# A weight stream in loads of two chunks with rows of 8 kB, in a two-block transformer kernel

## The reference

```python
sh1, sc1, gt1, sh2, sc2, gt2 = split(silu(c) @ w_mod + b_mod, 6)
h = rmsnorm(x, g_attn) * (1 + sc1) + sh1          # and the same for ctx
cq, ckv, kr, qn, kn, vn, f = split_columns(h @ w_in)
x = x + gt1 * (concat(o_mla, o_na, o_fn) @ w_out)
x = x + gt2 * conv_ffn(rmsnorm(x, g_ffn) * (1 + sc2) + sh2, w_up, w_down)
x = rmsnorm(x, g_final)
# second block
qa, ka, va, qb, kb, vb, ga, gb = split(rmsnorm(x) @ w_in_2)
x = x + (sigmoid(ga) * (ya @ w_branch_a_2) + sigmoid(gb) * (yb @ w_branch_b_2)) @ w_out_2
x = rmsnorm(x + swiglu(rmsnorm(x), w_ffn_in_2, w_ffn_down_2))
```

## Time and profile before

| | us |
|---|---|
| median of 3 runs | 2613.85 (2613.49 to 2614.14) |
| the profiled execution | 2613.18 |
| its span | 2611.3 |
| PE busy | 2589.2 (99%) |
| DVE busy | 1780.8 (68%) |
| ACT busy | 1219.5 (47%) |
| stream loads | 1016, 540.35 MB on their queue |
| read over the span | 209 GB/s |

### The profile page before, as it was taken

How to read it: one execution, slowest core, us unless ns; L and a number is a source line. 1 busy time by engine, 2 the same in 40 slices (tenths; PEclk the granted TensorE clock), 3 DMA queues, 4 the chain that set the end, 5 groups by cost and what they waited for, 6 DMA issues and landing times.

```text
span 2611.3 us, 37160 instructions
## 1 busy us (share of the span) xinstructions
PE 2589.2 (99%) x15234; PEld 2234.2 (86%) x15234; DVE 1780.8 (68%) x2469; ACT 1219.5 (47%) x1604; POOL 33.4 (1%) x30
## 2 busy tenths in 40 slices
PE   8999999999999999999999999999999999999999
PEld 5788778888888888888888888899888888888888
DVE  3377977888888877555656677676766666665555
ACT  4442445455555555444433555544444444444443
POOL 2100000000000000000000000000000000000000
PEclk9999999999999999999999999999999999999999
DMA  9887975667777655555555544465555555555553
GB/s 391 350 310 270 332 242 179 229 223 237 237 239 235 208 190 185 196 188 193 184 190 187 168 139 143 147 194 194 190 189 191 188 192 188 192 186 194 188 192 122
DMA packets 151561, 547.73 MB, mean 210 GB/s; under 512 B 16992, under 2 KB 18912, under 8 KB 150624
## 3 DMA queue, kind: packets, MB, share of 16 engines
q1 hardware_dynamic: 148752, 540.35, 61.2%
q10 hardware_dynamic: 2640, 5.01, 0.7%
HBM read 542.68 MB, written 2.10 MB: 209 GB/s over the span
## 4 chain that ended last, share of the span: by engine, by line
PE 92%; DVE 5%; DMA 2%; ACT 1%; issue 0%; SPq 0%; ACTq 0%; DVEq 0%
PE ps L481 47%; PE ps L480 24%; PE ps L478 3%; PE ps L485 3%; PE ps L486 3%; PE ps L487 3%; DVE lo L433 1%; DVE raw L444 1%; PE ps L479 1%; PE ps L493 1%; PE ps L492 1%; PE ps L491 1%; PE ps L1708 1%; DMA raw<-in_stream 1%; PE ps L1930 1%; DMA raw_deep<-in_stream 0%
## 5 line engine op out<-in xcount | busy, mean ns | idle before, releaser
L433 DVE TENSOR_TENSOR lo<-raw,hi 128x1024 fp32r<-128x1024 f32 x815 | 992.9, 1224 | 704.4 <-ACT hi L420 702.4
L481 PE MATMUL ps<-pair,hi 128*128 128x512 f32 x3994 | 1390.7, 392 | 0.0
L420 ACT ACTIVATE hi<-raw 128x1024 fp32r<-128x1024 f32 x815 | 860.4, 1059 | 1054.5 <-PE ps L481 894.1
L480 PE MATMUL ps<-pair,lo 128*128 128x256 f32 x3994 | 1119.4, 280 | 0.1
L481 PEld LDWEIGHTS ps<-pair,hi 128*128 128x128 f32 x3994 | 749.9, 188 | 161.2
L480 PEld LDWEIGHTS ps<-pair,lo 128*128 128x128 f32 x3994 | 749.9, 188 | 6.4 <-issue 2.8
L481 PE MATMUL ps<-hid,hi 128*128 128x512 f32 x1376 | 477.4, 392 | 0.0
L480 PE MATMUL ps<-hid,lo 128*128 128x256 f32 x1376 | 384.6, 280 | 0.0
L481 PEld LDWEIGHTS ps<-hid,hi 128*128 128x128 f32 x1376 | 258.3, 188 | 56.7
L480 PEld LDWEIGHTS ps<-hid,lo 128*128 128x128 f32 x1376 | 258.3, 188 | 0.3
L1298 DVE TENSOR_REDUCE tmp<-ps 128x256 f32<-128x512 f32 x260 | 176.6, 684 | 5.0 <-PE ps L481 4.6
(11 more groups left out here) (347 smaller groups left out, 2314.3 us busy)
## 6 DMA issues: line engine op xcount, KB each, us to landing
raw<-in_stream SPq DMA_DIRECT2D x983, 512.0 KB, 4.2
raw_deep<-in_stream SPq DMA_DIRECT2D x31, 512.0 KB, 10.7
xc<-in_xc SPq DMA_DIRECT2D x4, 1024.0 KB, 8.6
x<-in_x ACTq DMA_DIRECT2D x1, 2048.0 KB, 9.3
out<-out_sb SPq DMA_DIRECT2D x8, 256.0 KB, 2.9
c_bc<-in_c_bc SPq DMA_DIRECT2D x1, 1024.0 KB, 10.2
bias<-in_rpb ACTq DMA_DIRECT2D x4, 256.0 KB, 4.7
dft<-in_dft_tab ACTq DMA_DIRECT2D x1, 512.0 KB, 8.0
```

Of the source, the lines that this page charges most:

```text
L420: e.activation(hi[:, c % R, :], raw_of(p), ACT.Copy).then_inc(hi_ready, 1)
L433: e.tensor_tensor(lo[:, c % R, :], raw_of(p), hi[:, c % R, :].bitcast(F32), ALU.subtract)\
L480: e.matmul(out[:, T:2 * T], wlo, act[:, 0, :], start=False, stop=False)
L481: return e.matmul(out, whi, both_, start=False, stop=last)
```

## The change

The stream is laid out in pairs: rows 2t and 2t+1 of the list become one block of [128, 2048], so that each partition's row is 8 kB of contiguous memory. SP issues one DMA for two chunks (`load(t)`), into two neighbouring places, after waiting for both places to be free (`place_free`, twice). The places have one semaphore for two, and the users of both chunks wait for it. The order of chunks, the splits, the dots and the products stay. `N_DEEP` becomes 82, an even number, so that the second kr chunk also gets a place in the ring of 10. The kr chunks are now loaded whole. `vecs` is issued between chunks 3 and 4 and `c_bc` between 47 and 48, as before.

```diff
-N_DEEP = POS[("weights", AT[("a", KT - 1)])] + 1
+N_DEEP = (POS[("weights", AT[("a", KT - 1)])] + 2) // 2 * 2
...
-        landed = [sem(f"landed{i}") for i in range(RR + DEEP)]
+        landed = [sem(f"landed{i}") for i in range((RR + DEEP) // 2)]
...
-                e.wait_ge(landed[PLACE[p]], 16 * NTH[p])
+                e.wait_ge(landed[PLACE[p] // 2], 16 * NTH[p])
...
-            def load(p):
+            def place_free(p):
                 if PREV[p] is not None:
...
-                if SEQ[p][0] == "weights" and CHUNKS[SEQ[p][1]][0] == "kr":
-                    e.dma_start(raw_of(p)[:, 0:CH // 2], stream[p, :, 0:CH // 2]).then_inc(landed[PLACE[p]], 16)
-                else:
-                    e.dma_start(raw_of(p), stream[p]).then_inc(landed[PLACE[p]], 16)
-
+
+            def load(t):
+                p, n = 2 * t, min(2, len(SEQ) - 2 * t)
+                for k in range(n):
+                    place_free(p + k)
+                at = PLACE[p]
+                dst = raw[:, at:at + n, :] if at < RR else raw_deep[:, at - RR:at - RR + n, :]
+                e.dma_start(dst, stream[t, :, 0:n * CH].rearrange("p (s c) -> p s c", s=n)).then_inc(landed[at // 2], 16)
...
-            for p in range(4):
-                load(p)
+            for t in range(2):
+                load(t)
...
-            for p in range(4, 48):
-                load(p)
+            for t in range(2, 24):
+                load(t)
...
-            for p in range(48, len(SEQ)):
-                load(p)
+            for t in range(24, n_loads):
+                load(t)
...
+    out = out.reshape(-1, 2, P, CH).transpose(0, 2, 1, 3).reshape(-1, P, 2 * CH)
```

More of the change, by code:

```diff
@@ L527, in load @@
                         e.wait_ge(extra_used, i + 1)
-                if SEQ[p][0] == "weights" and CHUNKS[SEQ[p][1]][0] == "kr":
-                    e.dma_start(raw_of(p)[:, 0:CH // 2], stream[p, :, 0:CH // 2]).then_inc(landed[PLACE[p]], 16)
-                else:
-                    e.dma_start(raw_of(p), stream[p]).then_inc(landed[PLACE[p]], 16)
+            def load(t):
[5 more added lines that the diff above has]
+                e.dma_start(dst, stream[t, :, 0:n * CH].rearrange("p (s c) -> p s c", s=n)).then_inc(landed[at // 2], 16)
+            n_loads = (len(SEQ) + 1) // 2
             for i in range(4):
                 e.dma_start(xc[:, 4 * i:4 * i + 4], xc_d[:, 4 * i:4 * i + 4]).then_inc(s_xc[i], 16)
-            for p in range(4):
-                load(p)
+            for t in range(2):
+                load(t)
             e.dma_start(vecs[:], vecs_d).then_inc(s_vecs, 16)
-            for p in range(4, 48):
-                load(p)
+            for t in range(2, 24):
+                load(t)
             e.wait_ge(sqx_sum, 1)
@@ L2358, in lay_stream @@
     modT = np.ascontiguousarray(w_mod[:, 2 * D:].T)
-    out = np.zeros((len(SEQ), P, CH), np.float32)
+    out = np.zeros((2 * ((len(SEQ) + 1) // 2), P, CH), np.float32)
     def rows(w, k0, n, *cols):
```

## The result

The changed kernel takes 2620.93 us (median of 8 runs, 2618.83 to 2628.02), the kernel before beside it 2614.03; the ratio is 1.003, 95% interval [1.0021, 1.0038]. The forecast was 2616.1 with a range to 2620.5, so the loss is three times the forecast's (+6.9 against +2.3) and lies just outside the range. The profiled execution took 2619.49, 6.31 more than that of before.

The account below looks back on a forecast made before the run. PE's matmuls were taken to bound the kernel (busy 2589.2 of 2611.3 us). Terms 0.7 (start) - 0.2 (c_bc) + 0.6 (first-half weights) + 1.2 (fourth qn chunk) = +2.3 gave a median of 2616.1, range 2612.5 to 2620.5.

Parts of the forecast that it names:

- the faster rows: Stream queue: 8 kB rows at 418 against 409 GB/s gain 0.05 us a pair, 1.2 us by the c_bc load.

Follow-up runs that it names:

- land_pairs: Changed kernel, but each chunk issued alone once its own place is free, in 4 kB rows; both chunks of a pair still share one semaphore; 2618.86 us, ratio 1.0021.
- rope_early: Changed kernel with VectorE's two qrope_lo subtractions, and with them the copies to qeven and qodd, one split of ukv earlier; 2622.39 us, ratio 1.0034.
- clean_start: Changed kernel with pairs for positions 0 to 81 alone; other chunks singly, own semaphores, out of whole 512 kB blocks; 2616.58 us, ratio 1.0013.
- cbc_later: Changed kernel with c_bc and rope issued after pair 41 instead of after pair 24; 2619.34 us, ratio 1.0020.
- rows_4k: Changed kernel with the stream in its old DRAM layout, so a pair is one transfer of two blocks with 4 kB rows; 2622.49 us, ratio 1.0032.
- before_pitch: Kernel before with only the paired DRAM layout: chunks still loaded singly, as 4 kB rows lying 8 kB apart; 2616.92 us, ratio 1.0011.
- pairs_start: Changed kernel with pairs for chunks 0 to 81 alone; later chunks singly, own semaphores, as 4 kB rows out of the paired layout; 2619.29 us, ratio 1.0021.
- pairs_mid: Changed kernel with pairs for chunks 82 to 239 alone; other chunks singly, own semaphores, out of the paired layout; 2619.85 us, ratio 1.0020.

## What to carry to other kernels

Two transfers on one semaphore make the first consumer wait for the second transfer: 1.28 us here, where a landing is used at once. land_pairs, which has this and not the wait for two places, lost 5.4 us over the stages with no work stored up, while the saved issues and the faster rows bought nothing that the times show. Before a change that moves landings, list every wait of the bounding engine that is near zero and ends on something that hangs on the stream, over however many engines and queues: 0.2 us of wait is not "nothing", it is an edge. And when a layout changes along with a protocol, run the layout alone first: singles that carried it hid the cost of the pairs in four runs here.

## What the chip showed that I had not expected

- Transfers of 128 rows of 4 kB that lie 8 kB apart take a median of 4.6 us unqueued against 3.7 for one block, and the same 409 GB/s when queued. The Trainium skill (DMA: Bandwidth & Descriptors, Latency and other measured facts) has a loss of rate for row pitches of 2 MiB and more between HBM tensors; a loss of latency at 8 kB is another thing, and why it arises no run here shows.
- A pair of 1 MB lands in 4.8 us (median from 620 us on) with 8 kB rows and with 4 kB rows alike.
- A copy of 256 kB within SBUF takes 4.9 to 9.1 us while loads of the stream are queued (the second of the two, qodd, 6.4 to 9.1), and in rope_early the copy to qodd was issued 1.9 us earlier and landed 0.8 later.
- With 8 kB rows a pair issued while the one ahead of it had 3.3 to 4.0 us to go could land 3.9 to 4.5 us after it instead of 2.5 (pair 22 in the changed kernel, clean_start and cbc_later); with 4 kB rows it landed after 2.55 with 3.9 us to go (rows_4k). Why, no run here shows.
- PE's granted clock was 0.50 for a short stretch in different executions, at 24, 304 or 528 us, each time just behind a stage in which PE was idle in places. The length of the last idle time alone doesn't decide it: near 304 us the clock fell behind waits for qodd of 2.58 us (before_pitch) and 1.9 (pairs_start), and stayed at 1.00 behind 0.66 (the changed kernel), 1.78 (rope_early) and 3.0 (pairs_mid). It is also 0.50 behind the last matmuls of every trace, in the kernel before from 2608.9 us on, where it costs nothing.
